# Splitting each unit of twelve in the first projection into a product over 256 prompt tokens and one over 32 samples

## The chip, the core and the metric

The kernel runs on one core of a Trainium2 chip. The metric is the device time of one execution in microseconds; lower is better. The core's engines are TensorE (PE, with its weight loads shown apart as PEld), VectorE (DVE), ScalarE (ACT), GpSimd (POOL) and SyncE (SP), which run in parallel and wait for each other on semaphores.

## The reference

The computation is one inference step, two layers deep, for 256 prompt tokens and 8 x 4 = 32 sample tokens that share all weights. Each layer does:

```python
h = _rmsnorm(x, ln1)
z = h @ w_in                      # 1024 -> 7168: u, v, b, c, xin, gate_A, gate_B
u = gelu(u); v = _rmsnorm(gelu(v), ln_v)
ya = _chunk_gmlp(u, v, w_s, b_s) @ w_a
yc, conv_new = _short_conv(cg * xin, conv_prev, conv_w)
yb = (bg * yc) @ w_b
x = x + (sigmoid(ga) * ya + sigmoid(gb) * yb) @ w_o
x = x + _peer(_rmsnorm(x, ln2), w_q, k1, k2, u_tab, v_tab)   # 16384 one-neuron experts
x = x + sigmoid(_rmsnorm(x, ln3) @ w_pg) * (pe @ w_ple)
```

All arrays are float32. The changed part computes columns of `h @ w_in`: the v segment and the u segment.

## The kernel before

**Tiling.** Features lie on the 128 partitions and the T = 288 tokens along the free axis: columns 0 to 255 are the prompt, 256 to 287 the samples. All weights come as one stream of tiles of 128 x 1024, called units; four units make a quad. A unit of a projection yields 128 output features for all 288 tokens: it holds C = 8 blocks of 128 x 128 weights, one for each chunk of 128 input features.

**Precision.** Each float32 operand is split in two parts of the type fp32r: `w_hi` (rounded by ACT), `w_lo` (the rest, by DVE or POOL), and likewise `h_hi`, `h_lo` and `b_hi`, `b_lo` for the activations. `product` (lines 981 to 986) makes three matmuls for each block: w_hi x h_hi (L984), w_hi x h_lo (L985), w_lo x h_hi (L986), all accumulated in one PSUM bank `ps[:, j, 0:T]`. A unit is thus 8 x 3 = 24 matmuls of 128 x 128 weights against 288 columns. Every matmul loads its own weights, which the trace shows as LDWEIGHTS records on PEld, one for each matmul.

**Order on TensorE.** In each of the two layers TensorE walks through the quads in order. The first projection is quads 0 to 13. Quad 0 is `first_quad(0, ...)`, quads 1 to 3 are `segment(1, 3)`, a hardware loop of three passes with four units in each; quad 4 is `first_quad(4, ...)`, which in its first unit waits, chunk by chunk, for the normalised operand `b_lo`. Quads 0 and 1 give v, quads 2 and 3 give u. After quad 1 the loops of ACT and DVE carry more work for each unit, because they also make the operands `b_hi` and `b_lo` of the later quads.

**Waits of a unit.** A unit waits for `lo` (its weights' lower part is there) and for `evac` (its PSUM bank has been emptied), and its last matmul signals `mm`. On `mm` of a unit, ACT rounds the weights of the unit after the next (`split`, L385) and applies the gelu (L444), DVE scales the result with the inverse root into `z` (`evacuate`, L683), normalises a chunk of x (L664), makes `w_lo` of the unit after the next (L637) and, in quads 2 and 3, `b_lo` (L670). SP refills the four `raw` buffers as `lo` frees them. POOL adds up squares (L235) and prepares the mixing weights.

**Other products that the rows show.** L974 sums squares with a matrix of ones; L1030 transposes v; L1040, L1042 and L1044 are the token mixing, where L1044 multiplies 32 x 128 weights by 32 columns; L1112 builds the expert matrix from one-hot vectors. These are plain float32, and the trace shows two records for each of them other than the transposes.

Of the kernel before, what the change touches and what calls it, by code (L numbers as in the profile page):

```python
# [4 lines left out]
P = 128  # L5
DEPTH = 2
D = 1024
C = D // P
SEQ, DEC_B, DEC_S = 256, 8, 4
DEC = DEC_B * DEC_S  # L10
T = SEQ + DEC
# [51 lines left out]
def hybrid_trunk(nc, stream, x_in, pe_in, conv_in, gains_in, ws_in, ws_blk_in, bias_in, keys_in,  # L63
                 y_out, conv_out, v_out):
    ctx = ExitStack()
    with ctx:
        def sb(name, shape, dt, where=ctx):
            return where.enter_context(nc.sbuf_tensor(name, shape, dt))

        def sem(name):  # L70
            return ctx.enter_context(nc.semaphore(name))
# [5 lines left out]
        h_hi = sb("h_hi", [P, C, T], F32R)  # L77
        h_lo = sb("h_lo", [P, C, T], F32R)
# [52 lines left out]
        ps = ctx.enter_context(nc.psum_tensor("ps", [P, 8, 512], F32))  # L131
# [5 lines left out]
        lo = sem("lo")  # L137
        mm = sem("mm")
# [3 lines left out]
        evac = sem("evac")  # L142
        passed = sem("passed")
# [823 lines left out]
        def _(pe):  # L967
# [8 lines left out]
            with pe.Fori(0, DEPTH) as L:  # L976
                u0 = pe.snap(L * UNITS)
                e0 = pe.snap(L * EVACS)

                def product(out, j, col, rhs_hi, rhs_lo, first, last):  # L980

                    wh = w_hi[:, j % 2, col:col + P]
                    wl = w_lo[:, j % 2, col:col + P]
                    pe.matmul(out, wh, rhs_hi, start=first, stop=False)  # L984
                    pe.matmul(out, wh, rhs_lo, start=False, stop=False)  # L985
                    return pe.matmul(out, wl, rhs_hi, start=False, stop=last)  # L986

                def unit(q, j, evac_q, a_hi, a_lo):

                    pe.wait_ge(lo, u0 + q * 4 + (j + 1))  # L990
                    pe.wait_ge(evac, e0 + evac_q * 4 + (j + 1))
                    for c in range(C):
                        m = product(ps[:, j, 0:T], j, c * P, a_hi[:, c, :], a_lo[:, c, :], c == 0, c == C - 1)
                    m.then_inc(mm, 1)

                def segment(q_first, quads, a_hi=h_hi, a_lo=h_lo, skipped=0):
                    pe.sem_inc(passed, 1)
                    with pe.Fori(0, quads) as i:
                        for j in range(4):
                            unit(i + q_first, j, i + (q_first - skipped), a_hi, a_lo)  # L1000
# [5 lines left out]
                def first_quad(q, n, skipped=0, a_hi=h_hi, a_lo=h_lo, squares=None,  # L1006
                               order=range(C)):

                    for j in range(4):
                        pe.wait_ge(lo, u0 + (q * 4 + j + 1))  # L1010
                        pe.wait_ge(evac, e0 + ((q - skipped) * 4 + j + 1))
                        for k, c in enumerate(order):
                            if j == 0:
                                operand(n + k + 1)
                            m = product(ps[:, j, 0:T], j, c * P, a_hi[:, c, :], a_lo[:, c, :], k == 0, k == C - 1)
                        m.then_inc(mm, 1)
                        if j == 1 and squares is not None:
                            sum_squares(L * NORMS + squares, order[0])

                first_quad(0, 0, squares=1)  # L1020
                segment(1, 3)
                first_quad(4, C, a_hi=b_hi, a_lo=b_lo, squares=2)
                segment(5, 1, b_hi, b_lo)
                pe.wait_ge(t_ok, L * T_OPS + 2 * C)
                for k in range(3):
# [3 lines left out]
                    for c in range(C):  # L1029
                        m = pe.transpose(ps[0:n, 4 + (2 * k + c // 4) % 4, c % 4 * P:c % 4 * P + P],  # L1030
                                         t_op[:, c, k * P:k * P + n], ident[:, :])
                    m.then_inc(tr_ok, 1)
                segment(6, 2, b_hi, b_lo)
                pe.wait_ge(tok_ok, L * 3 + 3)
                pe.wait_ge(mixw_ok, L + 1)
# [21 lines left out]
                for r in range(ROUTES):  # L1057
# [3 lines left out]
                    for half in range(2):  # L1061
                        at = r % 2 * 2 * KEYS + half * KEYS
                        m = pe.matmul(ps[0:TT, 4 + g % 4, at:at + KEYS],
                                      z[:, 2 * head + half, tile * TT:tile * TT + TT], keys[:, half, :],
                                      start=True, stop=True)
# [21 lines left out]
                for k in range(3):  # L1087
                    for tile in range(NT):
                        m = pe.transpose(ps[:, 4 + k, tile * TT:tile * TT + TT],
                                         route[:, k, tile * HEADS:tile * HEADS + HEADS, :].rearrange("p r k -> p (r k)"),  # L1090
                                         ident[0:TT, 0:TT])
                m.then_inc(rT_ok, 1)
                fine_segment(U_TOP + U_ONLY - 1, 1)
                with pe.Fori(0, U_MIX) as i:
                    groups_at = [5, 10, 16, 21, 26, 31]
                    done, k = 0, 0
                    for j in range(4):
                        pe.wait_ge(lo, u0 + i * 4 + (4 * (Q_U + U_TOP + U_ONLY) + j + 1))
                        pe.wait_ge(evac, e0 + i * 4 + (4 * (Q_U + U_TOP + U_ONLY) + j + 1))
                        for c in range(C):  # L1100
                            m = product(ps[:, j, 0:T], j, c * P, h_hi[:, c, :], h_lo[:, c, :], c == 0, c == C - 1)
# [3 lines left out]
                            if done in groups_at:  # L1105

                                pe.wait_ge(g_used, L * N_GROUPS + i * PER_QUAD + (k + 1))
                                for t in range(GROUP):
                                    if t % 2 == 0:

                                        pe.wait_ge(hot_ok, 2 * (L * N_GROUPS + i * PER_QUAD) + (2 * k + t // 2 + 1))
                                    m = pe.matmul(ps[:, 4 + k % 2, t * P:t * P + P], hot2[:, t, :], hot1[:, t, :],  # L1112
                                                  start=True, stop=True)
# [22 lines left out]
                for j in range(4):  # L1136
# [7 lines left out]
                    for k in range(2):  # L1144
                        for c in range(CP):
                            m = product(ps[:, 4 + (2 * j + k) % 4, 0:T], j, (k * CP + c) * P,
                                        h_hi[:, 4 + c, :], h_lo[:, 4 + c, :], c == 0, c == CP - 1)
# [86 lines left out]
```

## Time and profile before

| | |
|---|---|
| Median of 2 runs | 2819.97 us (2819.18 to 2820.76) |
| Profiled execution's span | 2819.0 us; no time beside the span is shown for it |
| PE busy | 2594.6 us (92%) |
| PEld busy | 2529.6 us (90%) |
| DVE busy | 1968.1 us (70%) |
| ACT busy | 1150.6 us (41%) |
| POOL busy | 891.0 us (32%) |
| DMA | 393.34 MB, mean 140 GB/s |

Busy shares are averages over stages with different limits. Matmul ends are modelled, and a matmul's duration includes its way through the array, so successive matmuls overlap in the trace: the pace is read from the distance between their starts.

### The profile page before, as it was taken

What the parts mean: (1) busy time and instruction counts of PE and PEld (TensorE: products, weight loads), DVE (VectorE), ACT (ScalarE), POOL (GpSimd) and SP (SyncE); (2) the same over time, 40 slices, a digit from 0 to 9 for tenths busy, and PEclk for the clock granted to TensorE, in tenths of its full rate; (3) what the DMA queues carried; (4) which work ended last, traced back from release to release, by engine and by line L of the source; (5) the groups of instructions that cost most, each with busy time, mean ns of one, the idle gap of its engine ahead of it and who ended that gap; (6) DMA issues with size and microseconds to landing.
All of it is one profiled execution on the core that took longest, in us unless ns stands there. A gap on an engine that the chain in (4) does not pass through costs nothing.

```text
span 2819.0 us, 57289 instructions
## 1 busy us (share of the span) xinstructions
PE 2594.6 (92%) x18932; PEld 2529.6 (90%) x18932; DVE 1968.1 (70%) x3706; ACT 1150.6 (41%) x1844; POOL 891.0 (32%) x643
## 2 busy tenths in 40 slices
PE   8989999978888899999899899999788889999996
PEld 7889999978777899999898899999777778999996
DVE  6455779986999655544764567899789996554457
ACT  5434454432222344444653344544322223444445
POOL 2260159954434200000124400799543331000002
PEclk9989999989999999999998999999899999999998
DMA  5434544433222354444443445445322224444443
GB/s 183 129 114 165 175 141 164 160 115 112 82 89 89 128 167 166 164 164 165 157 151 107 137 164 179 137 164 164 111 97 86 85 86 150 165 164 164 165 166 111
DMA packets 108184, 393.34 MB, mean 140 GB/s; under 512 B 12624, under 2 KB 12816, under 8 KB 107600
## 3 DMA queue, kind: packets, MB, share of 16 engines
q1 hardware_dynamic: 105840, 384.02, 40.9%
q0 software_dynamic: 2272, 8.40, 0.8%
q8 instruction: 40, 0.66, 0.1%
q14 instruction: 32, 0.26, 0.0%
HBM read 388.42 MB, written 3.95 MB: 139 GB/s over the span
## 4 chain that ended last, share of the span: by engine, by line
PE 49%; issue 25%; POOL 18%; DVE 4%; ACT 2%; POOLq 1%; DVEq 0%; ACTq 0%; DMA 0%; SPq 0%
POOL w_lo L325 18%; PE ps L984 16%; PE ps L985 16%; PE ps L986 16%; DVE w_lo L637 1%; ACT w_hi L385 1%; DVE b_lo L676 1%; PE ps L1042 0%; PE ps L1040 0%; ACT b_hi L421 0%; DVE root L659 0%; DVE z L683 0%; ACT L412 0%; DVE b_lo L670 0%; POOLq L328 0%
## 5 line engine op out<-in xcount | busy, mean ns | idle before, releaser
L984 PE MATMUL ps<-h_hi,w_hi 128*128 128x288 f32 x4640 | 1390.5, 300 | 79.7 <-POOL w_lo L325 41.6
L985 PE MATMUL ps<-h_lo,w_hi 128*128 128x288 f32 x4640 | 1374.6, 296 | 0.0
L986 PE MATMUL ps<-h_hi,w_lo 128*128 128x288 f32 x4640 | 1372.6, 296 | 0.0
L637 DVE TENSOR_TENSOR w_lo<-raw,w_hi 128x1024 fp32r<-128x1024 f32 x472 | 614.7, 1303 | 628.7 <-ACT w_hi L385 626.7
L385 ACT ACTIVATE w_hi<-raw 128x1024 fp32r<-128x1024 f32 x568 | 601.3, 1059 | 1106.1 <-PE ps L986 1105.9
L984 PEld LDWEIGHTS ps<-h_hi,w_hi 128*128 128x128 f32 x4640 | 876.9, 189 | 85.1 <-POOL w_lo L325 42.1
L986 PEld LDWEIGHTS ps<-h_hi,w_lo 128*128 128x128 f32 x4640 | 878.1, 189 | 0.0
L985 PEld LDWEIGHTS ps<-h_lo,w_hi 128*128 128x128 f32 x4640 | 877.4, 189 | 0.0
L325 POOL TENSOR_TENSOR w_lo<-raw,w_hi 128x512 fp32r<-128x512 f32 (+1 forms) x416 | 687.2, 1664 | 585.7 <-ACT w_hi L385 356.9
L984 PE MATMUL ps<-b_hi,w_hi 128*128 128x288 f32 x1152 | 348.8, 303 | 23.6 <-DVE w_lo L637 21.6
L235 POOL TENSOR_TENSOR ext<-ext 128x288 f32<-128x288 f32 x63 | 57.1, 907 | 965.1 <-ACT ext L366 895.3
L985 PE MATMUL ps<-b_lo,w_hi 128*128 128x288 f32 x1152 | 346.6, 301 | 0.0
L986 PE MATMUL ps<-b_hi,w_lo 128*128 128x288 f32 x1152 | 346.0, 300 | 0.0
L1112 PE MATMUL ps<-hot 128*128 128x128 f32 x1152 | 190.6, 292 | 99.8 <-DVE hot L854 86.8
L1112 PEld LDWEIGHTS ps<-hot 128*128 128x128 f32 x1152 | 149.2, 190 | 139.2 <-DVE hot L854 139.1
L984 PEld LDWEIGHTS ps<-b_hi,w_hi 128*128 128x128 f32 x1152 | 223.3, 194 | 28.4 <-issue 22.9
L850 DVE TENSOR_TENSOR hot<-iota,routeT 128x256 f32<-128x256 f32 x288 | 211.7, 735 | 29.1 <-ACT mat L407 21.2
L985 PEld LDWEIGHTS ps<-b_lo,w_hi 128*128 128x128 f32 x1152 | 223.1, 194 | 0.3
L986 PEld LDWEIGHTS ps<-b_hi,w_lo 128*128 128x128 f32 x1152 | 222.9, 193 | 0.0
L854 DVE TENSOR_SCALAR hot<-iota,routeT 128x128 f32<-128x128 f32 x576 | 221.6, 425 | 0.0
L405 ACT ACTIVATE w_hi<-raw 128x512 fp32r<-128x512 f32 x160 | 101.6, 635 | 144.1 <-PE ps L986 144.1
L402 ACT ACTIVATE w_hi<-raw 128x512 fp32r<-128x512 f32 x160 | 101.3, 633 | 115.0 <-PE ps L986 115.0
(140 smaller groups left out, 1757.7 us busy)
## 6 DMA issues: line engine op xcount, KB each, us to landing
raw<-stream SPq DMA_DIRECT2D x730, 512.0 KB, 3.3
x_keep<-x POOLq DMA_DIRECT2D x2, 1152.0 KB, 6.4
x<-x_keep POOLq DMA_DIRECT2D x2, 1152.0 KB, 7.3
x<-x_in SPq DMA_DIRECT2D x4, 288.0 KB, 3.6
y_out<-t_op POOLq DMA_DIRECT2D x2, 576.0 KB, 3.1
ws<-ws_in POOLq DMA_DIRECT2D x2, 512.0 KB, 3.7
act_u<-pe_in POOLq DMA_DIRECT2D x2, 288.0 KB, 4.0
ws_blk<-ws_blk_in POOLq DMA_DIRECT2D x16, 0.5 KB, 3.0
```

The source lines that it names most:

```text
L235: a = pool.tensor_tensor(acc, acc, sq[:, order[k], :], ALU.add)
L325: return pool.tensor_tensor(w_lo[:, k % 2, lo_col:hi_col], raw[:, k, lo_col:hi_col], w_hi[:, k % 2, lo_col:hi_col].bitcast(F32), ALU.subtract)
L385: act.activation(w_hi[:, j % 2, :], raw[:, j, :], ACT.Copy).then_inc(hi, 1)
L402: act.activation(w_hi[:, k % 2, 0:D // 2], raw[:, k, 0:D // 2], ACT.Copy).then_inc(hi_half, 1)
L405: act.activation(w_hi[:, k % 2, D // 2:D], raw[:, k, D // 2:D], ACT.Copy).then_inc(hi, 1)
L637: dve.tensor_tensor(w_lo[:, j % 2, :], raw[:, j, :], w_hi[:, j % 2, :].bitcast(F32), ALU.subtract).then_inc(lo, 1)
L850: dve.tensor_tensor(hot2[:, k:k + 2, :], iota[:, :].unsqueeze(1).to_broadcast(grid), routeT[:, 1, bass.ds(g * GROUP + k, 2)].unsqueeze(2). ...
L854: h = dve.tensor_scalar(hot1[:, t, :], iota[:, :], routeT[:, 0, bass.ds(g * GROUP + t, 1)], routeT[:, 2, bass.ds(g * GROUP + t, 1)], ALU.i ...
L984: pe.matmul(out, wh, rhs_hi, start=first, stop=False)
L985: pe.matmul(out, wh, rhs_lo, start=False, stop=False)
L986: return pe.matmul(out, wl, rhs_hi, start=False, stop=last)
L1112: m = pe.matmul(ps[:, 4 + k % 2, t * P:t * P + P], hot2[:, t, :], hot1[:, t, :], start=True, stop=True)
```

## The change

`apart` takes the place of `segment` for quads 1 to 3 in both layers, which is 12 units in each. Within a unit, the same 24 products are first made over columns 0 to 255, and then the 24 again over columns 256 to 287, in the same PSUM bank. Waits and the signal `mm` stand where they stood: once for each unit, `mm` on the very last matmul. The other engines' programs are unchanged.

```diff
+                def apart(q_first, quads, a_hi=h_hi, a_lo=h_lo):
+
+                    pe.sem_inc(passed, 1)
+                    with pe.Fori(0, quads) as i:
+                        for j in range(4):
+                            pe.wait_ge(lo, u0 + (i + q_first) * 4 + (j + 1))
+                            pe.wait_ge(evac, e0 + (i + q_first) * 4 + (j + 1))
+                            for t0, t1 in ((0, SEQ), (SEQ, T)):
+                                for c in range(C):
+                                    m = product(ps[:, j, t0:t1], j, c * P, a_hi[:, c, t0:t1], a_lo[:, c, t0:t1],
+                                                c == 0, c == C - 1)
+                            m.then_inc(mm, 1)
...
                 first_quad(0, 0, squares=1)
-                segment(1, 3)
+                apart(1, 3)
                 first_quad(4, C, a_hi=b_hi, a_lo=b_lo, squares=2)
```

## Rows read from the trace of the kernel before

**Rows 1.** The page: the engines, and granted clock in 40 slices.

```profile
PE 2594.6 (92%) x18932; PEld 2529.6 (90%) x18932; DVE 1968.1 (70%) x3706; ACT 1150.6 (41%) x1844; POOL 891.0 (32%) x643
PEclk9989999989999999999998999999899999999998
```

**Rows 2.** The page: the chain that ended last, by engine.

```profile
PE 49%; issue 25%; POOL 18%; DVE 4%; ACT 2%; POOLq 1%; DVEq 0%; ACTq 0%; DMA 0%; SPq 0%
```

**Rows 3.** Windows of the changed stage, layers 1 and 2, and of each engine's busy time.

```profile
core 0: us, PE busy (x) PEld busy (x) DVE busy (x) ACT busy (x) POOL busy (x), PEclk, DMA share, GB/s
29.50:67.80 38.30, 38.30 (x287) 38.30 (x288) 27.98 (x38) 20.45 (x37) 6.81 (x8) 1.00 0.49 165
1424.10:1462.40 38.30, 38.30 (x287) 38.30 (x288) 28.82 (x38) 20.83 (x38) 6.88 (x8) 1.00 0.50 165
```

**Rows 4.** Groups by line from 29.5 to 67.8 us.

```profile
L984 PE MATMUL ps<-h_hi,w_hi 128*128 128x288 f32 x96 | 28.5, 297 | 1.5 <-DVE w_lo L637 1.5
L984 PEld LDWEIGHTS ps<-h_hi,w_hi 128*128 128x128 f32 x96 | 18.0, 187 | 1.7 <-issue 1.7
L637 DVE TENSOR_TENSOR w_lo<-raw,w_hi 128x1024 fp32r<-128x1024 f32 x12 | 14.7, 1225 | 3.6 <-ACT w_hi L385 3.3
L385 ACT ACTIVATE w_hi<-raw 128x1024 fp32r<-128x1024 f32 x11 | 11.7, 1061 | 17.0 <-PE ps L986 17.0
L683 DVE TENSOR_TENSOR z<-ps,root 128x288 f32 (+1 forms) x12 | 5.5, 456 | 6.7 <-PE ps L986 6.4
```

**Rows 5.** Timeline of the weight loads at 29.5 us: start, duration.

```profile
29.49 0.19 PEld L984 LDWEIGHTS ps<-h_hi,w_hi 128*128 128x128 f32 x1 [1.70 <-issue]
29.60 0.19 PEld L985 LDWEIGHTS ps<-h_lo,w_hi 128*128 128x128 f32 x1
29.73 0.19 PEld L986 LDWEIGHTS ps<-h_hi,w_lo 128*128 128x128 f32 x1
```

**Rows 6.** Timeline of the transposes and their loads, from 94 to 98 us.

```profile
94.63 1.91 PE L1030 MATMUL ps<-ident,t_op 128*128 128x128 f32 x16
94.51 1.80 PEld L1030 LDWEIGHTS ps<-ident,t_op 128*128 128x128 f32 x16
```

**Rows 7.** Timeline of weight loads around 32-column products, 127.9 and 133.0 us.

```profile
127.99 0.29 PEld L1044 LDWEIGHTS ps<-ws_blk,v_tok 32*128 32x128 f32 x2
128.21 0.19 PEld L1040 LDWEIGHTS ps<-bias,ones 1*128 1x128 f32 x1
133.01 0.50 PEld L1044 LDWEIGHTS ps<-ws_blk,v_tok 32*128 32x128 f32 x2 [0.22 <-issue]
133.39 0.33 PEld L1040 LDWEIGHTS ps<-bias,ones 1*128 1x128 f32 x1
```

**Rows 8.** Timeline of matmuls at the low clock, first unit of quad 0.

```profile
12.58 0.44 PE L986 MATMUL ps<-h_hi,w_lo 128*128 128x288 f32 x1
12.82 0.44 PE L984 MATMUL ps<-h_hi,w_hi 128*128 128x288 f32 x1
13.06 0.44 PE L985 MATMUL ps<-h_lo,w_hi 128*128 128x288 f32 x1
```

**Rows 9.** Windows around the token mixing, and the expert stage; columns as rows 3.

```profile
125.90:129.40 3.50, 3.50 (x20) 2.49 (x20) 3.50 (x1) 0.00 (x0) 3.50 (x2) 0.99 0.04 15
129.40:132.80 3.40, 3.07 (x10) 1.94 (x9) 2.24 (x5) 1.54 (x4) 3.17 (x6) 0.50 0.39 112
125.00:201.00 76.00, 68.51 (x396) 62.00 (x397) 40.83 (x30) 22.61 (x37) 58.47 (x57) 0.82 0.29 96
658.00:945.00 287.00, 238.76 (x1702) 219.50 (x1702) 275.94 (x542) 63.77 (x94) 112.93 (x47) 1.00 0.26 86
```

**Rows 10.** Timeline of matmuls at the end of quad 4's first unit.

```profile
70.64 0.29 PE L986 MATMUL ps<-b_hi,w_lo 128*128 128x288 f32 x1
71.43 0.40 PE L984 MATMUL ps<-b_hi,w_hi 128*128 128x288 f32 x1 [0.50 <-DVE b_lo L670]
```

## The prediction

> **What bounds the kernel now.** I began with the page. TensorE is busy for 92% of the span, at the full clock in most slices [rows 1], and the chain that ended last lies on PE for 49% and on "issue" for 25%, most of it the spacing between matmuls [rows 2]. The averages don't decide, so I took the changed stage by itself: quads 1 to 3, which run from 29.5 to 67.8 us in the first layer and from 1424.1 to 1462.4 us in the second. In both, PE is busy for all of the 38.30 us at a granted clock of 1.00, that is 2.4 GHz; DVE works 28 to 29 us of it, ACT 20 to 21, POOL 7, and the transfers take half of the DMA engines' time [rows 3]. So the stage is bound by TensorE, and whatever is added to its stream lengthens it.
>
> The pace: 12 units of 24 matmuls are 288 (287 in the trace, one record is missing), and 38.30 / 288 = 133.0 ns from start to start, 3.19 us for a unit. The engines that follow wait for PE, not the reverse: ACT stands idle for 17.0 us until PE has finished, DVE's evacuation for 6.4 us [rows 4]. DVE's 27.98 us are 2.3 us a unit, ACT's 20.45 are 1.7 us; both have room in a unit of 3.19 us and more in a longer one. The only wait of PE in the stage is at its head, 1.5 us for `w_lo` of L637 [rows 4]. It comes before the first changed product and stays.
>
> **What is removed and added.** Each of 24 units (12 in each layer) loses 24 matmuls of 288 columns and gets 24 of 256 and 24 of 32, and each of the 48 loads its own 128 x 128 weights. The column count is unchanged. The weight loads double: 24 x 24 = 576 more.
>
> *The wide product.* No fp32r matmul of 256 columns is in this trace. Its lower bound is the next row with as many passes of columns and a full weight load: 16 transposes of 128 float32 columns in 1.91 us, less 0.27 for the last one's way through the array, over 15, are 109 ns, with the loads beside them (1.80 - 0.19) / 15 = 107 ns apart [rows 6]. Its upper bound is the present product, 133 ns. At the low clock 288 columns take 240 ns [rows 8], which is exactly 288 / 1.2 GHz, so the column time is one cycle each; 32 columns less at 2.4 GHz are 13 ns, and 133 - 13 = 120 ns. I take 120, since the form of instruction is that of the 133 ns row and only the columns differ.
>
> *The narrow product.* 32 columns are 13 ns of columns, but a weight load has to come before each. How fast loads can follow each other: after the pause at the head of the stage, L984's load starts at 29.49 and L985's at 29.60, before the pace of the 288 columns takes hold (the next is at 29.73) [rows 5]. That is 110 ns. The nearest row in columns says the same: around L1044, with 128 columns of weights and 32 columns that stream, two loads later is 128.21 - 127.99 = 0.22 us, 110 ns each [rows 7]. The lower bound is 107 [rows 6], and the upper 133: the narrow product keeps whatever makes the wide one slower than its columns (288 columns at 2.4 GHz would be 120, the row says 133). I take 109, nearest to both rows.
>
> By the Trainium skill ("TensorE: Matmul & The Clock Gate", LDWEIGHTS) a load takes its columns / 1.2, here 107 ns; the rows agree at 107 to 110. The same page's section on the back-to-back gap has another rule, which speaks against all of this: N / 2.4 + 2.5 ns for a single product and a floor near 25 ns for narrow ones, so 109 + 25 = 134 ns in place of 122.5. This would give hardly any change, and is weighed among the rivals by what rows say of it.
>
> *The unit at full clock:* 24 x (120 + 109) = 5.50 us, against 3.19. The extra is 2.31 us; 24 units make 55.4 us, 27.7 in each layer. With both bounds low (24 x 216 = 5.18 us) it is 48 us, with both high (24 x 266 = 6.38) 77 us.
>
> *The clock.* Here the narrow half matters twice. It is 24 x 109 = 2.6 us in each unit in which the array gets 13 ns of columns every 109. The trace shows such work once in each layer: between 125.9 and 129.4 us PE is shown busy throughout, with token mixing that has 32-column products and products with few rows among full ones, and after it the granted clock is 0.50, that is 1.2 GHz, with only a little idle time shown. In the expert stage, 658 to 945 us, PE is idle more (238.76 of 287 us busy), but what it does is full matmuls of 288 and 128 columns, and the clock stays at 1.00 [rows 9]. So a busy PE record does not hold the clock, and the narrow half resembles the first of the two. At 1.2 GHz the wide product takes 256 / 1.2 = 213 ns (by the 240 for 288 [rows 8]), the narrow one by its load: 133.01 to 133.39 for two [rows 7] is 190 each, twice 109 is 218; either way everything in the stage goes at half speed. The share of time at the low level I take from the nearest stretch that alternates between thin and full work, 125 to 201 us: mean granted clock 0.82 [rows 9], which is (1 - 0.82) / 0.5 = 36% of the time at the low level. 12 units of full-clock work are 66.0 us; at a mean of 0.82 they take 80.5 us. Extra in a layer: 80.5 - 38.3 = 42.2 us; in two, 84.4 us. Bounds: no fall (55), and low for half of the time, 66.0 / 0.75 = 88 us, 99 us extra in two layers.
>
> *What lies around.* The loop body grows from 96 to 192 matmuls, so six passes might wait for their instructions. Before, the passes show nothing (PE busy all through [rows 3]); I take 0, and as bound the one "issue" gap of the stage, 1.7 us [rows 4], at each of four jumps back: 7 us. Behind the stage PE stops for about 0.66 us, at 70.64 to 71.43 less one spacing, for DVE's last `b_lo` [rows 10]. That is DVE's chain after the last unit's signal; it stays, at most it vanishes because DVE comes rested (1.3 us less in two layers). The semaphores, the evacuations and the DMA issues are as many as before; the transfers only get more time. Later stages shift as a whole.
>
> **Sum.** 2819.0 (the span; the median of the runs is 1 us above it, and no time outside the span is given) + 84.4 = **2903 us**.
>
> **The rivals.**
>
> *A. The clock holds* (chance 0.27). Narrow and wide alternate every 2.6 and 2.9 us, and the expert stage shows that PE may have gaps without a fall [rows 9]; a narrow fp32r product may also occupy the array for longer than 13 ns, unseen behind its load. Then 2819 + 55 = 2874, 2867 to 2881 with 216 to 240 ns a pair.
>
> *B. The forecast* (0.43): 2903, with its own range 2885 to 2918.
>
> *C. The narrow product costs as much as a wide one* (0.09): 133 ns for both, no matter how many columns. For it: 13 ns in the present pace that the columns don't explain. At full clock 77 us, 2896; at a clock of 0.82 (12 x 6.38 / 0.82 = 93.4; 55.1 a layer), 2929.
>
> *D. Narrow fp32r products run like plain float32 ones* (0.06): two records each, 220 ns with two loads. Unit 24 x 340 = 8.16 us, extra 4.97 x 24 = 119 us, 2938 at full clock and about 3000 with the clock falling.
>
> *E. Not slower: only columns count* (0.13). If the second load of the same weights is hidden or left out by the hardware, a pair is 120 + 13 = 133 ns and nothing changes: 2819; with a floor of 25 ns, 24 x 12 ns x 24 units = 7 us, 2826. It decides as soon as a load takes less than some 25 ns when its weights were in the array lately. Against it: L984 and L985 already use the same weights one after the other, and the load of L985 is there with 0.19 us like every other [rows 5]; and loads never stand closer than 107 ns in rows 5 to 7.
>
> *F. Anything else* (0.02), such as an earlier end of a stall that I've not seen. That the change does not do what it says I hold for nothing: the calls are plain.
>
> **How the numbers follow.** The predicted time is B's, 2903. The range 2866 to 2935 holds A, B and C, 0.79. A change of 2% (56.4 us, to 2876.4) is about what a measurement of this kernel can tell from none. Slower by over 2%: B 0.43, C 0.09, D 0.06, and a third of A, 0.09: 0.67. Within 2%: two thirds of A 0.18, E 0.12, rest 0.01: 0.31. Faster by over 2%: 0.02.
>
> **What would show it.** PE records rise by 576 and so do PEld's. In the stage, starts of 256-column products 118 to 121 ns apart and of 32-column ones 107 to 112 ns at full clock; PEld's starts show the load as the pace of the second. The window of the first layer's stage is 66 us if A is right, about 80 with a granted clock near 0.82 if B is. ACT and DVE busy sums are unchanged, their waits for L986 longer. Narrow starts 13 to 27 ns apart would show E; 133 C; two records for each narrow product D. I would be wrong altogether if PE did not bound the stage: then the stage would lengthen by less than the sum of its matmuls.

## The result and the profile after

The changed kernel takes 2902.85 us (median of 2 runs, 2901.43 to 2904.26) against 2819.97 before: a ratio of 1.029, 95% interval 1.0275 to 1.0314. It is slower by 83 us, and the forecast was 2903. In the later comparisons the kernel before lay between 2811.75 and 2821.66 us, so differences of a few microseconds say little.

The page of the changed kernel, engines and granted clock, in answer to [rows 1]:

```profile
PE 2680.0 (92%) x19508; PEld 2616.6 (90%) x19508; DVE 1967.6 (68%) x3706; ACT 1150.7 (40%) x1844; POOL 891.0 (31%) x643
PEclk8889999999999999999989899999899999999998
```

PE and PEld have 576 records more each, as they must. DVE, ACT and POOL work as long as before. Of the clock's digits, those of slices 1, 2 and 21 fell, where the changed stage stands; the 8 in slice 3 was there before.

Windows of the changed kernel: the stage of each layer (in answer to [rows 3]), then two short stretches inside the first. The columns are those of [rows 3].

```profile
30.60:110.70 80.10, 80.04 (x577) 80.05 (x577) 29.70 (x38) 20.43 (x37) 7.18 (x8) 0.81 0.26 86
1466.80:1546.90 80.10, 80.08 (x577) 80.08 (x577) 28.87 (x38) 20.80 (x38) 7.19 (x8) 0.81 0.25 85
36.20:42.50 6.30, 6.30 (x56) 6.30 (x56) 2.14 (x3) 1.97 (x3) 0.00 (x0) 1.00 0.24 83
42.50:46.00 3.50, 3.50 (x19) 3.50 (x18) 1.23 (x1) 0.81 (x2) 0.00 (x0) 0.52 0.22 49
```

The stage grew from 38.30 to 80.10 us in both layers, 83.6 us in all, and the spans differ by 2902.8 - 2819.0 = 83.8 us. So the difference lies in the 24 changed units: the rest of the span differs by 0.2 us in sum (the first stage starts 1.1 us later, what follows each stage is 0.2 and 0.7 us shorter). PE is all but never idle in them, yet the mean clock is 0.81: from 42.5 us on it is at the low level for 3.5 us, though PE's busy share did not change.

Groups by line in the first stage, in answer to [rows 4]: ACT's and DVE's work is nearly as before (1299 ns in place of 1225 for a `w_lo`), and their waits for PE grew, from 17.0 to 54.7 us and from 6.4 to 43.3.

```profile
L984 PE MATMUL ps<-h_hi,w_hi 128*128 128x256 f32 (+1 forms) x192 | 58.6, 305 | 1.5 <-DVE w_lo L637 1.5
L637 DVE TENSOR_TENSOR w_lo<-raw,w_hi 128x1024 fp32r<-128x1024 f32 x12 | 15.6, 1299 | 3.7 <-ACT w_hi L385 3.3
L385 ACT ACTIVATE w_hi<-raw 128x1024 fp32r<-128x1024 f32 x11 | 11.7, 1060 | 54.7 <-PE ps L986 54.7
L683 DVE TENSOR_TENSOR z<-ps,root 128x288 f32 (+1 forms) x12 | 5.5, 457 | 43.3 <-PE ps L986 43.3
```

The timeline of PE in the changed kernel (start, duration): narrow products, then wide ones at full clock, then wide ones at the low clock.

```profile
35.75 0.26 PE L986 MATMUL ps<-h_hi,w_lo 128*128 128x32 f32 x1
35.86 0.26 PE L984 MATMUL ps<-h_hi,w_hi 128*128 128x32 f32 x1
35.98 0.26 PE L985 MATMUL ps<-h_lo,w_hi 128*128 128x32 f32 x1
...
36.40 0.28 PE L985 MATMUL ps<-h_lo,w_hi 128*128 128x256 f32 x1
36.52 0.28 PE L986 MATMUL ps<-h_hi,w_lo 128*128 128x256 f32 x1
...
43.00 0.41 PE L986 MATMUL ps<-h_hi,w_lo 128*128 128x256 f32 x1
43.21 0.41 PE L984 MATMUL ps<-h_hi,w_hi 128*128 128x256 f32 x1
43.42 0.41 PE L985 MATMUL ps<-h_lo,w_hi 128*128 128x256 f32 x1
```

Narrow starts are 112 ns apart, wide ones 119 at full clock and 213 at the low one. A row's own duration is longer, since successive products overlap. And the loads of the narrow stretch, on PEld:

```profile
35.84 0.19 PEld L984 LDWEIGHTS ps<-h_hi,w_hi 128*128 128x128 f32 x1
35.95 0.19 PEld L985 LDWEIGHTS ps<-h_lo,w_hi 128*128 128x128 f32 x1
36.06 0.19 PEld L986 LDWEIGHTS ps<-h_hi,w_lo 128*128 128x128 f32 x1
```

They follow each other at the same 0.11 us as the narrow products, L984 and L985 too, which load the same weights.

### The profile page after: what moved, and what is told of

The parts are those of the page before. It is cut to its first block, busy times and chain, and to the rows that moved or that the text cites. A ratio compares the mean times of both kernels' runs of the same rounds, so it can differ in the third digit from the quotient of the medians.

```text
span 2902.8 us, 58441 instructions
## 1 busy us (share of the span) xinstructions
PE 2680.0 (92%) x19508; PEld 2616.6 (90%) x19508; DVE 1967.6 (68%) x3706; ACT 1150.7 (40%) x1844; POOL 891.0 (31%) x643
## 4 chain that ended last, share of the span: by engine, by line
PE 51%; issue 24%; POOL 18%; DVE 4%; ACT 2%; POOLq 1%; DVEq 0%; DMA 0%; ACTq 0%; SPq 0%
POOL w_lo L325 18%; PE ps L984 17%; PE ps L985 16%; PE ps L986 16%; DVE w_lo L637 1%; ACT w_hi L385 1%; DVE b_lo L676 0%; PE ps L1055 0%; PE ps L1053 0%; DVE root L659 0%; ACT b_hi L421 0%; ACT L412 0%; DMA raw<-stream 0%; DVE z L683 0%; POOLq L328 0%
## 5 line engine op out<-in xcount | busy, mean ns | idle before, releaser
L984 PE MATMUL ps<-h_hi,w_hi 128*128 128x288 f32 (+1 forms) x4832 | 1449.9, 300 | 79.6 <-POOL w_lo L325 41.6
L985 PE MATMUL ps<-h_lo,w_hi 128*128 128x288 f32 (+1 forms) x4832 | 1433.9, 297 | 0.0
L986 PE MATMUL ps<-h_hi,w_lo 128*128 128x288 f32 (+1 forms) x4832 | 1432.2, 297 | 0.0
L984 PEld LDWEIGHTS ps<-h_hi,w_hi 128*128 128x128 f32 x4832 | 927.6, 192 | 84.3 <-POOL w_lo L325 42.1
L986 PEld LDWEIGHTS ps<-h_hi,w_lo 128*128 128x128 f32 x4832 | 928.4, 192 | 0.0
L985 PEld LDWEIGHTS ps<-h_lo,w_hi 128*128 128x128 f32 x4832 | 928.2, 192 | 0.0
L984 PE MATMUL ps<-b_hi,w_hi 128*128 128x288 f32 x1152 | 349.5, 303 | 21.8 <-DVE w_lo L637 20.8
L985 PE MATMUL ps<-b_lo,w_hi 128*128 128x288 f32 x1152 | 347.5, 302 | 0.0
L984 PEld LDWEIGHTS ps<-b_hi,w_hi 128*128 128x128 f32 x1152 | 224.0, 194 | 26.0 <-issue 20.7
L985 PEld LDWEIGHTS ps<-b_lo,w_hi 128*128 128x128 f32 x1152 | 224.0, 194 | 0.3
```

## The experiments

The theory has two terms. **Loads:** a narrow product costs its weight load. **Clock:** a stretch of narrow products lowers TensorE's clock although PE is busy. The rivals to tell apart are that narrow products cost by their number in some other way, that the load of weights already in the array is free, and that products with few columns are slow by themselves. The cuts of code below are shortened, and all are against the changed kernel.

**Control for the other bank.** The interleaved kernels below need a second PSUM bank for the samples.

```diff
-    m = product(ps[:, j, t0:t1], j, ...)
+    m = product(ps[:, j if t0 == 0 else 5 + j % 2, t0:t1], j, ...)
```

> As the change, but the 32 sample columns of quads 1 to 3 are accumulated in another PSUM bank (5 or 6), and the evacuation does not read them: the samples' part of v and u is left out. It is the control for the two kernels that follow, which need that bank. Both theories expect no difference from the changed kernel: about 2903 us, wide products 119 and narrow ones 112 ns apart at full clock, and the clock alternating in the stage.

Measured: 2902.58 us, ratio 1.0296 (1.0277 to 1.0316). The other bank makes no difference, nor does it that nobody reads the samples' part.

**Wide and narrow interleaved.**

```diff
-    for t0, t1 in ((0, SEQ), (SEQ, T)):
-        for c in range(C): (three products)
+    for c in range(C):
+        for w, a in ((w_hi, a_hi), (w_hi, a_lo), (w_lo, a_hi)):
+            for t0, t1 in ((0, SEQ), (SEQ, T)):
+                m = pe.matmul(ps[:, j if t0 == 0 else 5 + j % 2, t0:t1], w[...], a[...], ...)
```

> The same 48 products of each unit with the same operands, but each narrow one stands right behind the wide one with the same weights, so that thin work never stands together; the samples go to the other bank and are not read, as in the control. Theory S (it is the thin stretch of 2.7 us in each unit that costs the clock): clock 1.00 all through the stage, a pair takes 118 + 112 = 230 ns, the unit 5.53 us, 24 x (5.53 - 3.19) = 56 us more than before, 2876 us. Rival N (576 more loads and products cost the clock by their number, or each costs more than the trace's spacing tells): 2903 us as the change. Rival E (a second load of the same weights right behind the first is free): a pair near 135 ns, 2820 us.

**Even halves.**

```diff
-    for t0, t1 in ((0, SEQ), (SEQ, T)):
+    for t0, t1 in ((0, T // 2), (T // 2, T)):
```

> The change with the cut at column 144 in place of 256: 24 products over columns 0 to 143, then 24 over 144 to 287, the full result. Theory S with loads as the pace: 144 columns are 60 to 67 ns, less than a load, so every product takes 112 ns, the unit 48 x 0.112 = 5.38 us, no thin stretch, clock 1.00: 24 x 2.19 = 52 us, 2872 us. Rival: products of less than 256 columns run several times slower for each column, hidden behind the load at 32 columns only: with four times the column time 240 ns each, 11.5 us a unit, 3019 us.

The profiled executions took 2866.28 us (interleaved) and 2867.05 us (even halves). Their windows of the first layer's stage, interleaved and then even:

```profile
29.00:95.40 66.40, 66.40 (x577) 66.40 (x578) 28.76 (x38) 20.45 (x37) 6.19 (x8) 1.00 0.30 103
```

```profile
28.80:93.20 64.40, 64.36 (x576) 64.37 (x577) 28.80 (x38) 20.43 (x37) 6.55 (x8) 1.00 0.31 106
```

In these two executions theory S is met: the same 48 products and loads in a unit as the change, in 66.4 us instead of 80.1, at a clock of 1.00. The spans are 10 and 5 us below what was expected; the stages are not, the rest of the program was shorter, and no run shows why. The load of the same weights right behind itself is not free (a pair is 230 ns, not 135), and 144 columns are no slower each than 256: 112 ns, the pace of the load. But each kernel was run three more times, and those took 2927.21 to 2930.45 us and 2924.03 to 2928.90 us, with mean clocks of 0.955 to 0.957 in place of 0.978 and 0.977. In those the interleaved kernel is slower than the change. This had not been expected and gave a new question: the same program has two times, 57 to 64 us apart. The tests with a low head below show, for the even halves, what the second one can be.

**The prompt alone.**

```diff
-    for t0, t1 in ((0, SEQ), (SEQ, T)):
+    for t0, t1 in ((0, SEQ),):
```

> Quads 1 to 3 multiply the 256 prompt tokens alone; the 24 narrow products are left out, so v and u of the samples are not computed. It measures the wide product by itself. If columns pace it (118 to 119 ns): unit 2.84 us, 24 x 0.35 = 8 us less than before, 2812 us, clock 1.00. If the load with something fixed on top paces 288 and 256 columns alike (133 ns), 2820 us.

Measured: 2812.26 us, ratio 0.9978 (0.9963 to 0.9992); the stage is 34.50 us at a clock of 1.00:

```profile
30.30:64.80 34.50, 34.46 (x288) 34.41 (x288) 27.33 (x38) 20.90 (x37) 5.63 (x8) 1.00 0.53 183
```

That is 24 products in 34.50 / 12 = 2.88 us, pauses included, and 119 ns from start to start. 32 columns less are 14 ns less than the 133 before, so columns pace the wide product.

**Eight narrow products in place of 24.**

```diff
-    for t0, t1 in ((0, SEQ), (SEQ, T)):
-        for c in range(C): (three products)
+    for c in range(C): (three products over columns 0:SEQ)
+    for c in range(C):
+        m = pe.matmul(ps[:, j, SEQ:T], w_hi[:, j % 2, c * P:c * P + P], a_hi[:, c, SEQ:T], ...)
```

> The change, but the narrow half of a unit is 8 products (high parts only) in place of 24, so 16 x 24 = 384 narrow products are left out, and the samples' v and u have lower precision. Theory S: the thin stretch is 8 x 112 = 0.9 us, too short to lower the clock; unit 24 x 118.5 + 8 x 112 = 3.74 us; against the prompt-only kernel 192 products x 112 ns = 21.5 us more, 2834 us, clock 1.00 in the stage. Rival E2 (a product of 32 columns costs only its columns or an issue of 25 ns, the rest was the clock): 2812 + 5 = 2817 us.

Measured: 2832.14 us, ratio 1.0043 (1.0026 to 1.006). The window of the stage:

```profile
29.20:74.30 45.10, 45.03 (x385) 45.03 (x385) 28.85 (x38) 20.45 (x37) 6.42 (x8) 1.00 0.44 140
```

It has 12 x 8 = 96 narrow products, which cost (45.10 - 34.50) / 96 = 110 ns each. The clock has no part in it, and the load term stands by itself.

**Narrow products with small weights.**

```diff
-    for t0, t1 in ((0, SEQ), (SEQ, T)):
-        for c in range(C): (three products)
+    for c in range(C): (three products over columns 0:SEQ)
+    for c in range(C): (for each of the three pairs w, a)
+        m = pe.matmul(ps[0:32, j, SEQ:T], w[:, j % 2, c * P:c * P + 32], a[:, c, SEQ:T], ...)
```

> The change with 24 narrow products in each unit, but their weights are 128 rows x 32 columns in place of 128 x 128: three quarters of the samples' features in v and u are left out. The number of products and the 32 columns that stream stay. Theory L (the load of 128 columns of weights is what a narrow product costs, 112 ns): the load shrinks to about a quarter, a narrow product to about 28 ns, the thin stretch to 0.7 us, clock 1.00: unit 24 x (118.5 + 28) = 3.52 us, 2812 + 24 x 24 x 0.028 = 2828 us. Rival (any narrow product costs 112 ns, whatever it loads): as the change, 2903 us with the clock alternating.

Measured: 2826.59 us, ratio 1.0033 (1.0022 to 1.0043); the stage is 44.60 us at a clock of 1.00. Its window, and the timeline of PE in it (L1008 is the narrow product in this kernel):

```profile
28.70:73.30 44.60, 44.52 (x577) 44.28 (x577) 28.81 (x38) 20.44 (x37) 6.71 (x8) 1.00 0.43 142
...
31.70 0.18 PE L1008 MATMUL ps<-h_hi,w_hi 128*32 128x32 f32 x1
31.73 0.18 PE L1008 MATMUL ps<-h_lo,w_hi 128*32 128x32 f32 x1
31.76 0.18 PE L1008 MATMUL ps<-h_hi,w_lo 128*32 128x32 f32 x1
```

As many products of as many columns, but 30 ns apart instead of 112, (44.60 - 34.50) / 288 = 35 ns each with the turns between wide and narrow. So a narrow product has no fixed price of 112 ns, and neither its number nor its 32 columns make it slow. This edit also narrows the product's output from 128 rows to 32, which it can't tell from the smaller load. That it is the load rests on PEld's spacing of 0.11 us and on the even halves, where 144 columns take the same 112 ns. The Trainium skill ("TensorE: Matmul & The Clock Gate", "Back-to-back issue gap") has a floor of about 25 ns for narrow products; the 30 ns with small weights are near to it, and the 112 ns with full weights are over four times as long.

**Four shorter stretches.**

```diff
-    for t0, t1 in ((0, SEQ), (SEQ, T)):
-        for c in range(C):
+    for half in range(2):
+        for t0, t1 in ((0, SEQ), (SEQ, T)):
+            for c in range(4 * half, 4 * half + 4):
```

> All 48 products of a unit, but in four stretches: 12 wide, 12 narrow, 12 wide, 12 narrow (samples in the other bank and not read, as in the control with the other bank). Theory S with the length of the thin stretch (1.3 us in place of 2.7): clock 1.00 in the stage when it starts high, unit 5.53 us, 2876 us; an execution that finds the clock low at the head may keep it low in part, up to 2930. Rival N (the number of thin products counts): 2903 us, as the change, with the clock alternating.

Measured: 2872.92 us (2871.47 to 2873.98), ratio 1.0185 (1.0168 to 1.0202). Its window of the first stage:

```profile
29.00:95.50 66.50, 66.41 (x576) 66.42 (x577) 28.84 (x38) 20.43 (x37) 6.20 (x8) 1.00 0.32 103
```

Against the control with the other bank (2902.58 us) only the order of the 48 products differs, and 30 us of 83 are gone, with the clock's fall; all four executions show it. So the clock term does not come from the number of narrow products but from their order: 24 together, 2.7 us, cost it, and 12 together, 1.3 us, did not.

**A low clock made at the head, and what follows it.** Three kernels begin quad 1 of each layer with the same thin work; behind it stand the kernel before, the even halves, and the change.

```diff
+    for _ in range(40):
+        pe.matmul(ps[:, 7, 0:32], ones[:, :], ones[:, 0:32], start=True, stop=True)
     segment(1, 3)        (the kernel before; apart(1, 3) in the other two)
```

> The kernel before, with a low clock made at the head of quad 1 of each layer: 40 plain float32 products of 32 columns with full weights (80 records, 80 weight loads) into an unused PSUM bank, then quads 1 to 3 as before. The result is unchanged. Both theories: PE shows no idle time in the thin part, yet the clock falls to 0.50 in it, and the 80 records take 9 us at 112 ns or up to 17 at 214. The 288-column products then start at 240 ns apart and return to 133 within a few us (about 2 us lost). 13 to 17 us more in each layer, 2846 to 2852 us. It is the control for the next kernel. If the clock stays at 1.00 through the thin part, the thin work is not what lowers it and the explanation of the change's second term falls.

> The even halves (48 products of 144 columns in each of the 24 units) behind the same thin head. Theory K (at the low clock a load takes 214 ns and the 144 columns behind it are too thin to bring the clock back, so it stays low as long as the stage lasts): every product of the stage 214 ns apart, a stage of 123 us in place of 64, in both layers; against the control 2 x (123 - 40) = 166 us more, 3012 us or so. Rival R (the clock returns as in the control, and the 2924 us of three of four executions of the even halves have another cause): 2 x 26 = 52 us more than the control, about 2900 us.

> The change itself behind the thin head of the control (40 plain products of 32 columns with full weights before quad 1; full result). Theory K: at the low clock the wide half of 24 x 213 ns = 5.1 us brings the clock back by itself, so the change does not stay low like the even halves did; stage 80 to 84 us in both layers, 2 x (82 - 40) = 84 us above the control's 2842, 2926 us. Rival: it stays low for the whole stage, as the even halves: 24 x 24 x 0.427 = 246 us in two stages, 3008 us.

Measured: 2842.05 us (before, 1.0077, interval 1.0057 to 1.0098), 3010.91 us (even halves, 1.0676, 1.0655 to 1.0698) and 2929.54 us (the change, 1.0398, 1.0367 to 1.0429). The kernel before with the head is 22 us slower, below the 26 to 32 us expected: the head's 80 records took 11.7 us in the first layer, 44 of them still at full clock, and 1.5 us of that would have been a wait. Windows of it: the head, the 3.5 us after it, and then the stage.

```profile
29.00:39.50 10.50, 10.50 (x68) 10.50 (x68) 1.74 (x3) 0.70 (x2) 1.49 (x2) 0.69 0.31 100
39.50:43.00 3.50, 3.50 (x17) 3.50 (x17) 0.00 (x0) 0.00 (x0) 0.00 (x0) 0.50 0.02 5
43.00:78.00 35.00, 35.00 (x263) 35.00 (x263) 25.04 (x34) 18.93 (x34) 3.88 (x5) 1.00 0.42 142
```

PE is busy throughout, and the clock falls in the thin work all the same; under the 288-column products that follow it is back within 3.5 us. The windows of the stage behind the same head, first the even halves and then the change:

```profile
39.40:162.30 122.90, 122.90 (x578) 122.90 (x578) 27.38 (x36) 19.97 (x36) 4.70 (x6) 0.50 0.14 47
```

```profile
39.40:123.30 83.90, 83.90 (x578) 83.90 (x577) 27.39 (x36) 19.97 (x36) 4.73 (x6) 0.76 0.21 69
```

In the even halves the clock stays at the low level for the whole of 122.9 us, and in the second layer for 122.8 us. Their timeline at 80 us shows the products at the pace of the slow loads:

```profile
79.83 0.41 PE L984 MATMUL ps<-h_hi,w_hi 128*128 128x144 f32 x1
80.04 0.41 PE L985 MATMUL ps<-h_lo,w_hi 128*128 128x144 f32 x1
80.25 0.41 PE L986 MATMUL ps<-h_hi,w_lo 128*128 128x144 f32 x1
```

With 144 columns every 214 ns the clock did not come back; with 256 every 213 in the change's wide half it did, again and again. This gives the even halves two times: 64.4 us for a stage that finds the clock high, 122.9 for one that finds it low. One stage of two held low is 58.5 us more, 2867.05 + 58.5 = 2925.6, and three of its four executions lay within 3.3 us of that. Their mean clocks agree: 0.957 and 0.955 in place of 0.977 are 119 to 132 us more at the low level. That one stage was low in just those executions is inferred from these two sums, since none of them has a trace. What the interleaved kernel's three slower executions were was not tested; their clocks and times are alike, and no more is shown.

**512 columns.**

```diff
-    for t0, t1 in ((0, SEQ), (SEQ, T)):
-        for c in range(C): (three products)
+    for c in range(C):
+        n = 512 if c < C - 1 else T
+        m = product(ps[:, j, 0:n], j, c * P, flat a_hi[c * T:c * T + n], flat a_lo[...], ...)
```

> The kernel before with 512 columns in place of 288 in 21 of a unit's 24 products of quads 1 to 3 (chunks 0 to 6; the columns beyond 288 are surplus, read from the next chunk, and nobody reads their result; the result is full). It measures what paces a wide fp32r product at full clock, where 288 columns take 133 ns in place of the 120 of one column a cycle, and 256 take 118.5. If each column costs 133 / 288 = 0.462 ns: 236 ns, and 21 x 24 x 0.103 = 52 us more than before, 2872 us. If a fixed 13 ns is added to one cycle a column: 227 ns, 47 us more, 2867 us; the spacing in the trace tells the two apart.

Measured: 2862.5 us, ratio 1.016 (1.0131 to 1.0189).

```profile
30.93 0.40 PE L984 MATMUL ps<-h_hi,w_hi 128*128 128x512 f32 x1
31.16 0.39 PE L985 MATMUL ps<-h_lo,w_hi 128*128 128x512 f32 x1
31.39 0.40 PE L986 MATMUL ps<-h_hi,w_lo 128*128 128x512 f32 x1
```

Starts are 231 to 232 ns apart, between the two expectations (227 and 236), so neither a fixed part nor a price for each column alone describes 119, 133 and 232 ns for 256, 288 and 512 columns. A fixed 6 ns and 0.442 ns for each column together fit all three, but three points do not test this, and why it is so stays open; for the change it moves one term by 1 ns.

## Why the prediction was right

**The bound.** The stage was PE's: both stages together grew by 83.6 us, the spans by 83.8.

**The wide product.** Taken at 120 ns; 119 in the changed kernel's timeline and in the prompt-only kernel.

**The narrow product.** Taken at 109 ns from the load spacing; 112 in the timeline, 110 by the difference of stages in the kernel with eight of them. Rivals C (133), D (two records, 220) and E (only columns) are refuted by the same rows, and so is the floor of 25 ns for this product. The sum at full clock was 55.4 us; the four stretches, which have the load term alone, show 2 x (66.5 - 38.3) = 56.4 us of stage.

**The clock.** 29 us were forecast for it. It is 2 x (80.1 - 66.5) = 27.2 us by the stages (30 by the medians): rival A, the holding clock, was wrong, and the four stretches show what it would have looked like. The mean clock was taken as 0.82 from the token mixing and its surroundings; it was 0.81. Two parts of that step were still off. The prediction let everything in the stage run at half speed, the narrow products too; in fact the low level falls on the wide half (213 ns), and the narrow ones stay at 112, because the fall comes at the end of the thin stretch or just after it and the rise before the next one. A wide product goes from 119 to 213 ns, a factor of 1.79 and not 2, so the same share of low clock costs less: 66.5 / 0.81 would be 82.1 us, and the stage took 80.1. And the stretch from 125 to 201 us, with its stalls and its few-row products, has no inner reason to give the same share; that 0.82 and 0.81 agree is luck. The bounds with and without a fall, 55 to 99 us in all, were what the rows supported. That 2903 was met to within a microsecond is luck too: the full-clock sum was 1.0 us too low and the clock term 1.8 us too high.

**What lies around.** The larger loop body costs nothing visible: PE is busy for 80.04 of 80.10 us. The wait for the last `b_lo` in quad 4's first unit [rows 10], which the sum left in place, is gone from the list of waits, in both layers. The clock is low from the unit's start in the first layer and from 1 us into it in the second, so its products take longer and DVE is in time; in the first layer:

```profile
110.67 0.53 PE L984 MATMUL ps<-b_hi,w_hi 128*128 128x288 f32 x1
111.00 0.44 PE L985 MATMUL ps<-b_lo,w_hi 128*128 128x288 f32 x1
111.24 0.44 PE L986 MATMUL ps<-b_hi,w_lo 128*128 128x288 f32 x1
```

## What to carry to other kernels

Cutting the moving operand does not cut a product's price in proportion when each product loads its own weights: below the load's time (here 112 ns at full clock, a little less than the 119 of 256 columns) every piece costs a load. Price such a split twice, by the loads it adds and by how long thin products stand together, because a busy PE does not by itself hold its clock. If a split is needed, alternate wide and narrow pieces in groups: 12 and 12 kept the clock in all four executions (2871 to 2874 us), while strict alternation, one and one, took 2927 to 2930 us in three of four, more than the change itself. And look at whether a stage can climb back from the low clock: one in which loads set the pace may stay low for its whole length, as the even halves did, and then the program has two times.

## What the runs showed of the hardware that had not been expected

- A stream can stay at the low clock: behind the same head, 288-column products were back at full clock within 3.5 us, 144-column ones stayed at 214 ns for 122.9 us, in both layers of the traced execution; the other took as long (3010.34 and 3011.48 us).
- In the changed kernel the clock falls nearly once in each unit: 18 of 24 units take 6.9 to 7.2 us, with most of the wide half at 213 ns and the narrow products at 112, and the other six take 5.5 us.
- An fp32r product costs more than one cycle a column at 2.4 GHz (119, 133 and 232 ns for 256, 288 and 512 columns, where 107, 120 and 213 would be one), but one at 1.2 GHz (213 and 240 ns for 256 and 288).
